# First projections of a hybrid backbone step: two blocks of 1024 channels and three column chunks, or four blocks of 512 and four chunks

## The chip, the cores and the metric

One NeuronCore of one Trainium2 chip runs the whole step in one launch. The metric is the device time of that launch in microseconds. TensorE (PE) multiplies into eight PSUM banks of 128 x 512 fp32, ScalarE (ACT) and VectorE (DVE) work between PSUM and the on-chip memory, GpSimd (POOL) and SyncE (SP) mainly issue DMAs; 16 DMA engines serve all queues.

## What is computed

Two sequences of 128 tokens (context and latent, `NS = 2`) go through one layer at D = 2048, in float32. Cut to what matters here:

```python
mod = silu(cvec) @ w_ada + b_ada            # 2048 x 12288, split in six: shift1, scale1, gate1, shift2, scale2, gate2
h = rmsnorm(x, g1) * (1 + scale1) + shift1
p = h @ w_in + b_in                          # 2048 x 8192: u (1024) | q | k | v (3 x 1024) | gate_A | gate_B (2 x 2048)
A = fourier(u) @ w_fourier;  B = attention(q, k, v, cached keys) @ w_na_o
x = x + gate1 * ((sigmoid(gate_A) * A + sigmoid(gate_B) * B) @ w_out)
x = x + gate2 * hierarchical_moe(modulate(x))    # 16 experts, 2048 -> 512 -> 2048
```

## The kernel before

**The weights' ring.** All of w_ada, w_in, w_na_o, w_fourier and w_out come in loads of 1 MB into `raw`, a ring of `RAW = 4` slots, in one fixed order (`ring_order`), issued by SP. A load waits until the slot four loads earlier is released (`slot_released`, on `raw_done`). There are two kinds. An ada load is consumed by PE directly: four fp32 products of the conditioning vectors with 512 columns each (`ada_block`, L685, for shift1 and scale1; `ada_super`, L701, for the four later sixths), 8 records in the trace. A dense load `l` is four rows-of-128 of a projection weight by 512 columns; ACT rounds it to fp32r (`high(u)`, L1257: `w_hi`), DVE takes the rest (`low(u)`, L1599: `w_lo = raw - w_hi`, which releases the slot after the second half), and PE multiplies in two units, `unit(l, 0)` and `unit(l, 1)`, of 12 matmuls each (three products L719 to L721 for two k and two sequences). `w_hi` and `w_lo` have four places (`AHEAD = 4`): high(u) waits for unit u - 4. A product adds up in a pair of PSUM banks over all loads of a chunk of 512 columns; then `read_chunk` on DVE (L1677) adds the bias row and writes it to `uqkv`.

**The first projections.** h needs shift1 and scale1, and these need every row of w_ada for their columns. The kernel before makes them in two blocks of 1024 channels: 16 ada loads, the evacuation of the rows (`modrow`, ACT, L1310), `mod_block` (PE turns the rows into columns, L734; DVE adds and scales), `modulate` (ACT, L1296, four instructions for four k of a sequence) and `split_h` (DVE, L1633 and L1634: h_hi and h_lo). While block 1's ada loads run, three to each dense load, the products of block 0 run: loads 0 to 5 are the two quads of k that are ready, for three column chunks (`P0_CHUNKS = 3`). The three sums stay open in six banks until loads 6 to 11 add the other half; each of these comes with one load of the later sixths (`ada_super`). From `L_MAIN = 12` on every chunk runs through its four quads, with one ada_super load to each dense load as long as there are any, and the rest hangs on `l`: attention heads at `HEAD_AT` (15, 17, 19, 21, 25, 27, 29, 31), the Fourier mixing at `DFT_AT` = 33, the columns of shift2 at DFT_AT + 6, the gates and merges from `L_MERGE` = 32, w_out from `L_OUT` = 80 to `L_ALL` = 96.

**After the ring** come the router and the 16 experts in eight pairs, whose loads (mraw) can begin when the ring's last dense loads are used up (SP waits on `unit_used`).

**POOL's queue** is a fixed list too: two bias rows of w_in (`load_bin`) once half of h is there (`h_ready` 4), then after `h_ready` 8 the relative-offset bias (eight small loads, `bias_rows` out to memory, four `bias` blocks back), two heads' cached keys and values (`cst`), and the further bias rows, each when the row before it in its place has been added.

## Time and profile before

| | us |
|---|---|
| Median of three runs | 1265.59 (1264.56 to 1265.74) |
| The profiled execution | 1263.68 |
| Its span, first to last instruction | 1261.9 |
| PE busy, DVE busy, ACT busy | 1156.0, 511.2, 373.8 |
| Moved by DMA | 423.27 MB |

Durations are of the profiled execution. A fp32 matmul has two records, and matmuls overlap, so that 24 matmuls of a dense load take less than 24 times the mean of one; times from start to start are the ones to add up.

### The profile page before, as it was taken

The numbers are of one execution on the slowest core, as the hardware profiler recorded it, in microseconds if no ns is written. First come the engines' busy times: TensorE is split into PE (matmuls) and PEld (weight loads), VectorE is DVE, ScalarE is ACT, GpSimd is POOL, SyncE is SP. The second block draws the span as 40 slices with busy tenths as digits, with TensorE's granted clock in tenths as the row PEclk, the third lists the DMA queues.
The fourth block names the chain that finished last, engine by engine and source line by source line (L and its number), as shares of the span: only waits on it lengthen the run. The fifth ranks groups of instructions, "written<-read, shape, count | busy, mean of one in ns | idle before, by whom it ended". The sixth has DMA issues, their size and how long they took to land.

```text
span 1261.9 us, 14226 instructions
## 1 busy us (share of the span) xinstructions
PE 1156.0 (92%) x5577; PEld 685.2 (54%) x5577; DVE 511.2 (41%) x722; ACT 373.8 (30%) x530; POOL 44.3 (4%) x81
## 2 busy tenths in 40 slices
PE   5779899999999999999999999999798889888785
PEld 2236567766766676778887784444233324333232
DVE  0022445545533445546456646125133323323046
ACT  3222424433332333334445534221021111201013
POOL 0000210010000300000000000000000000000000
PEclk9689899999999999999999999999999999999998
DMA  9999999888774998886565558999999999999998
GB/s 379 407 376 354 323 327 360 289 315 286 280 268 161 327 320 310 319 281 206 179 249 185 174 193 345 421 422 419 422 421 421 421 421 421 421 421 420 421 408 322
DMA packets 105955, 423.27 MB, mean 335 GB/s; under 512 B 8865, under 2 KB 9041, under 8 KB 73121
## 3 DMA queue, kind: packets, MB, share of 16 engines
q1 hardware_dynamic: 101264, 410.55, 84.8%
q0 software_dynamic: 4032, 11.22, 2.9%
q8 instruction: 45, 0.74, 0.2%
q10 hardware_dynamic: 592, 0.59, 0.1%
q14 instruction: 22, 0.17, 0.0%
HBM read 418.37 MB, written 3.95 MB: 335 GB/s over the span
## 4 chain that ended last, share of the span: by engine, by line
PE 69%; DMA 27%; DVE 1%; ACT 1%; issue 1%; SPq 0%; DVEq 0%; POOL 0%; ACTq 0%
PE bank L719 14%; PE bank L721 13%; PE bank L720 13%; PE bank L1086 11%; DMA raw<-in_w_ada 8%; DMA mraw<-in_w_exp_up 6%; DMA mraw<-in_w_exp_gate 5%; PE bank L701 4%; DMA mraw<-in_w_exp_down 4%; PE bank L1116 3%; DMA mraw_g<-in_w_exp_up 2%; PE bank L1027 2%; PE bank L685 2%; DMA mraw_g<-in_w_exp_down 1%; PE bank L1157 1%; PE bank L865 1%
## 5 line engine op out<-in xcount | busy, mean ns | idle before, releaser
L1599 DVE TENSOR_TENSOR w_lo<-raw,w_hi 128x1024 fp32r<-128x1024 f32 x192 | 233.6, 1224 | 273.7 <-ACT w_hi L1257 273.2
L1257 ACT ACTIVATE w_hi<-raw 128x1024 fp32r<-128x1024 f32 x192 | 201.9, 1058 | 312.8 <-PE bank L721 221.4
L1086 PE MATMUL bank<-mraw,xg 128*64 128x512 f32 x904 | 233.5, 601 | 18.2 <-DMA mraw<-in_w_exp_gate 8.0
L719 PE MATMUL bank<-w_hi,h_hi 128*128 128x512 f32 x512 | 210.7, 411 | 3.9 <-DVE w_lo L1599 3.9
L721 PE MATMUL bank<-w_hi,h_lo 128*128 128x512 f32 x512 | 201.4, 393 | 0.0
L720 PE MATMUL bank<-w_lo,h_hi 128*128 128x512 f32 x512 | 201.4, 393 | 0.0
L1086 PEld LDWEIGHTS bank<-mraw,xg 128*64 128x64 f32 x904 | 73.5, 137 | 137.3 <-issue 133.4
L1116 PE MATMUL bank<-mraw,hidT 128*64 128x512 f32 x408 | 101.1, 596 | 24.2 <-DMA mraw<-in_w_exp_down 22.0
L719 PEld LDWEIGHTS bank<-w_hi,h_hi 128*128 128x128 f32 x512 | 97.3, 190 | 47.5 <-issue 29.2
L721 PEld LDWEIGHTS bank<-w_hi,h_lo 128*128 128x128 f32 x512 | 97.2, 190 | 21.5
L720 PEld LDWEIGHTS bank<-w_lo,h_hi 128*128 128x128 f32 x512 | 97.5, 190 | 19.5 <-issue 1.0
L1545 ACT ACTIVATE d_hi<-bank,slot_w 128x512 fp32r<-128x512 f32 x32 | 22.0, 687 | 237.4 <-PE bank L1116 149.4
L2007 DVE SCALAR_TENSOR_TENSOR d_lo<-bank,slot_w,d_hi 128x512 fp32r<-128x512 f32 x32 | 23.9, 747 | 167.7 <-ACT d_hi L1545 167.0
L1116 PEld LDWEIGHTS bank<-mraw,hidT 128*64 128x64 f32 x408 | 32.5, 136 | 82.6 <-issue 75.9
L685 PE MATMUL bank<-raw,cpad 128*32 128x512 f32 x256 | 44.9, 789 | 32.9 <-DMA raw<-in_w_ada 32.9
L2019 DVE TENSOR_TENSOR bank<-bank,ga2b 128x512 f32<-128x512 f32 x64 | 41.5, 694 | 80.3 <-PE bank L1157 80.2
L701 PE MATMUL bank<-raw,cpad 128*32 128x512 f32 x512 | 67.4, 604 | 2.9 <-DMA raw<-in_w_ada 2.9
L1086 PE MATMUL bank<-mraw_g,xg 128*64 128x512 f32 x120 | 54.7, 598 | 3.2 <-DMA mraw<-in_w_exp_gate 3.1
L719 PE MATMUL bank<-w_hi,m_hi 128*128 128x512 f32 x128 | 51.5, 402 | 0.0
L721 PE MATMUL bank<-w_hi,m_lo 128*128 128x512 f32 x128 | 50.0, 391 | 0.0
L720 PE MATMUL bank<-w_lo,m_hi 128*128 128x512 f32 x128 | 49.9, 390 | 0.0
L1954 DVE TENSOR_TENSOR xg<-bank,rbi 128x512 f32<-128x512 f32 x32 | 21.9, 685 | 52.9 <-PE bank L1027 52.5
(260 smaller groups left out, 1140.7 us busy)
## 6 DMA issues: line engine op xcount, KB each, us to landing
raw<-in_w_in SPq DMA_DIRECT2D x64, 1024.0 KB, 5.8
raw<-in_w_ada SPq DMA_DIRECT2D x64, 1024.0 KB, 7.4
mraw<-in_w_exp_up SPq DMA_DIRECT2D x59, 1024.0 KB, 16.0
mraw<-in_w_exp_gate SPq DMA_DIRECT2D x58, 1024.0 KB, 16.0
mraw<-in_w_exp_down SPq DMA_DIRECT2D x51, 1024.0 KB, 16.0
raw<-in_w_ada SPq DMA_DIRECT2D x64, 512.0 KB, 7.9
raw<-in_w_out SPq DMA_DIRECT2D x16, 1024.0 KB, 5.0
raw<-in_w_na_o SPq DMA_DIRECT2D x8, 1024.0 KB, 5.4
```

Of the source, the lines that this page charges most:

```text
L685: last = nc.tensor.matmul(bank[7 - b % 2][32 * g:32 * g + 32], cpad[:, j], raw[:, n % RAW, g], start=j == 0, stop=j == KD - 1)
L701: last = nc.tensor.matmul(bank[7][32 * g:32 * g + 32], cpad[:, k], raw[:, n % RAW, g], start=k == 0, stop=k == KD - 1)
L719: nc.tensor.matmul(o, hi[:, k, s], wh, start=k == 0, stop=False)
L720: nc.tensor.matmul(o, hi[:, k, s], wl, start=False, stop=False)
L721: last = nc.tensor.matmul(o, lo[:, k, s], wh, start=False, stop=k == LOAD_K * quads - 1)
L1027: last = nc.tensor.matmul(out[:, kk * EPG * CAP:(kk + 1) * EPG * CAP], (t_hi, t_lo)[part][:, s, k * P:(k + 1) * P], pick[:, s, g * EPG:(g ...
L1086: last = nc.tensor.matmul(out[x * CAP:(x + 1) * CAP], xg[:, q * LOAD_K + kk, e * CAP:(e + 1) * CAP], slab(slot)[:, kk * COL:(kk + 1) * COL ...
L1116: last = nc.tensor.matmul(bank[first_bank + n][x * CAP:(x + 1) * CAP], hidT[:, i % 2, k, x * CAP:(x + 1) * CAP], slab(slot)[:, n * COL:(n ...
L1257: nc.scalar.activation(w_hi[:, u % AHEAD], r, ACT.Copy).then_inc(hi_ready, 1)
L1599: v.tensor_tensor(w_lo[:, u % AHEAD], r, w_hi[:, u % AHEAD].bitcast(F32), ALU.subtract).then_inc(raw_done[n % RAW], 4)
L2007: v.scalar_tensor_tensor(out=d_lo[:, c % 2], in0=bank[first_bank + n][:], scalar=slot_w[:, i:i + 1], in1=d_hi[:, c % 2].bitcast(F32), op0= ...
L2019: v.tensor_tensor(bank[out + s][:], bank[out + s][:], ga2b[:, s, cols], ALU.mult).then_inc(y_scaled, 1)
```

## The change

The first projections run in four blocks (`BLOCKS = 4`) of 512 channels, one quad of k each, for four column chunks (`P0_CHUNKS = 4`). A block takes 8 ada loads, each of two rows of k by 512 columns of shift1 and scale1 (the same 1 MB, in pieces of 2 KB where they were 4 KB). Between the blocks' dense loads (four to a block) stand the ada loads of the next block. Each dense load is now a sum of its own, opened and closed in a pair of banks; two pairs take turns, and `add_partial` on DVE adds it to `uqkv` in memory (the first with the bias row), 16 of these for the 16 dense loads. PE waits for the add of load l - 2 before load l. h of sequence 0 is modulated on ACT, that of sequence 1 on DVE. `L_MAIN` is 16; the number of loads in all stays the same, 96 ada and 96 dense. The heads follow one another without a break (17, 19, ... 31), the columns of shift2 come at 44, the evacuations of the later sixths 8 loads later, the mask is added at L_MAIN + 1 instead of L_MAIN + 3, and GpSimd loads four bias rows early (`xT_ready` 6). Counts of reads become `reads(chunk) = chunk + 1 + 12`.

```diff
-        P0_CHUNKS = 3
+        P0_CHUNKS, BLOCKS = 4, 4
         L_MAIN = 4 * P0_CHUNKS
-        L_MERGE = L_MAIN + 4 * 5
+        L_MERGE = L_MAIN + 4 * (8 - P0_CHUNKS)
         L_OUT = L_MERGE + 4 * 12
         L_ALL = L_OUT + 4 * 4
         A_SUPER = 32
-        A_MAIN = A_SUPER + 7
+        A_MAIN = A_SUPER + 3
...
-        ring_order = ["ada"] * 16 + ["ada", "ada", "ada", "dense"] * 5 + ["ada", "dense"]
-        ring_order += ["ada"] + ["ada", "dense"] * 6
+        ring_order = ["ada"] * 8 + ["dense"]
+        for b in range(BLOCKS - 1):
+            ring_order += ["ada", "ada", "ada", "dense"] * 2 + ["ada", "ada", "dense", "dense"]
+        ring_order += ["ada", "dense"] * 3
...
-            pair = chunk if chunk < P0_CHUNKS else (chunk - P0_CHUNKS) % 2
+            pair = (chunk + 1) % 2
             return 2 * pair, 2 * pair + 1
 
+        def reads(chunk):
+            return chunk + 1 + 3 * P0_CHUNKS
         def x1T_bank(n, s):
 
             return 1 if n == 3 and s else 6
 
-        HEAD_AT = [L_MAIN + 3 + 2 * h for h in range(4)] + [L_MAIN + 13 + 2 * h for h in range(4)]
+        HEAD_AT = [L_MAIN + 1 + 2 * h for h in range(8)]
         DFT_AT = HEAD_AT[7] + 2
+        SHIFT_AT = max(DFT_AT + 6, super_end(SHIFT2) + 2)
...
-                n = ADA_AT[16 * b + j]
+                n = ADA_AT[8 * b + j]
                 slot_released(n)
                 for m in (SHIFT1, SCALE1):
-                    sp.dma_start(raw[:, n % RAW, 2 * m:2 * m + 2].rearrange("p (a k) n -> p a (k n)", a=1),
-                                 ada_v[:, j:j + 1, m * D + b * 2 * COL:m * D + (b + 1) * 2 * COL]).then_inc(raw_landed[n % RAW], 16)
+                    sp.dma_start(raw[:, n % RAW, 2 * m:2 * m + 2],
+                                 ada_v[:, 2 * j:2 * j + 2, m * D + b * COL:m * D + (b + 1) * COL]).then_inc(raw_landed[n % RAW], 16)
...
-            for j in range(16):
+            for j in range(8):
                 ada_block_load(0, j)
-            for i in range(6):
-                for j in range(3 * i, min(3 * i + 3, 16)):
-                    ada_block_load(1, j)
-                dense_load(i)
-            ada_super_load(A_SUPER)
-            for i in range(6):
-                ada_super_load(A_SUPER + 1 + i)
-                dense_load(6 + i)
+            dense_load(0)
+            for b in range(1, BLOCKS):
+                for ch, js in ((1, (0, 1, 2)), (2, (3, 4, 5)), (3, (6, 7))):
+                    for j in js:
+                        ada_block_load(b, j)
+                    dense_load(P0_CHUNKS * (b - 1) + ch)
+                dense_load(P0_CHUNKS * b)
+            for i in range(3):
+                ada_super_load(A_SUPER + i)
+                dense_load(L_MAIN - 3 + i)
...
-            pool.wait_ge(h_ready, 4)
+            pool.wait_ge(xT_ready, 6)
             load_bin(0)
             load_bin(1)
+            load_bin(2)
+            load_bin(3)
             pool.wait_ge(h_ready, 8)
             load_bias_rows()
             load_cached_head(0)
             load_cached_head(1)
             skew_bias_rows()
-            load_bin(2)
-            load_bin(3)
...
-                n = ADA_AT[16 * b + j]
+                n = ADA_AT[8 * b + j]
                 if j == 0 and b == 1:
                     pe.wait_ge(vecT_ready, 1)
+                if j == 0 and b >= 2:
+                    pe.wait_ge(mod_ready, b - 1)
                 pe.wait_ge(raw_landed[n % RAW], landed_count(n))
                 for g in range(4):
-                    last = nc.tensor.matmul(bank[7 - b % 2][32 * g:32 * g + 32], cpad[:, j], raw[:, n % RAW, g],
-                                            start=j == 0, stop=j == KD - 1)
+                    last = nc.tensor.matmul(bank[7 - b % 2][32 * g:32 * g + 32], cpad[:, 2 * j + g % 2], raw[:, n % RAW, g],
+                                            start=j == 0, stop=j == 7)
...
-            def unit(l, half):
+            def unit(l, half, within=None):
 
                 chunk, quad, quads = chunk_of(l)
+                first, final = (LOAD_K * quad, LOAD_K * quad + 3) if l < L_MAIN else (0, LOAD_K * quads - 1)
...
+                    if t and within is not None:
+                        mod_block(within)
...
-                if quad == 0 and chunk >= P0_CHUNKS:
-                    pe.wait_ge(chunk_read, chunk - 2 if chunk < P0_CHUNKS + 2 else chunk - 1)
+                if l < L_MAIN:
+                    if l >= 2:
+                        pe.wait_ge(chunk_read, l - 1)
+                elif quad == 0:
+                    pe.wait_ge(chunk_read, reads(chunk - 2))
...
-            for j in range(1, 16):
+            for j in range(1, 8):
                 ada_block(0, j)
                 if j == 2:
                     pe.wait_ge(diag_ready, 1)
-                if 2 <= j < 10:
-                    if j >= 8:
-                        pe.wait_ge(xT_ready, j - 7)
-                    norm_transpose(x0, j - 2, bank[(j - 2) % 6])
+                if j >= 2:
+                    norm_transpose(x0, j - 2, bank[j - 2])
             mod_block(0)
-            for j in range(3):
-                ada_block(1, j)
-            for i in range(6):
-                for j in range(3 * i + 3, min(3 * i + 6, 16)):
-                    ada_block(1, j)
-                if i == 0:
-                    pe.wait_ge(xT_ready, 8)
-                    pe.wait_ge(h_ready, 2)
-                if i == 3:
-                    pe.wait_ge(h_ready, 4)
-                unit(i, 0)
-                if i == 5:
-                    mod_block(1)
-                unit(i, 1)
-            ada_super(A_SUPER)
-            ada_super(A_SUPER + 1)
-            for i in range(6):
-                ada_super(A_SUPER + 2 + i)
-                if i == 5:
-                    ada_super(A_SUPER + 8)
-                if i == 0:
-                    pe.wait_ge(h_ready, 6)
-                if i == 3:
-                    pe.wait_ge(h_ready, 8)
-                unit(6 + i, 0)
-                unit(6 + i, 1)
+            for b in (6, 7):
+                pe.wait_ge(xT_ready, b - 5)
+                norm_transpose(x0, b, bank[b - 6])
+            pe.wait_ge(xT_ready, 8)
+            def next_ada(b, js):
+                for j in js:
+                    if b < BLOCKS:
+                        ada_block(b, j)
+                    else:
+                        ada_super(A_SUPER + j)
+            for b in range(BLOCKS):
+                l = P0_CHUNKS * b
+                last_block = b == BLOCKS - 1
+                pe.wait_ge(h_ready, 2 * b + 2)
+                banks_free(l)
+                unit(l, 0)
+                next_ada(b + 1, (0,))
+                unit(l, 1)
+                next_ada(b + 1, (1,) if last_block else (1, 2))
+                banks_free(l + 1)
+                unit(l + 1, 0)
+                next_ada(b + 1, (2,) if last_block else (3,))
+                unit(l + 1, 1)
+                next_ada(b + 1, () if last_block else (4, 5))
+                banks_free(l + 2)
+                unit(l + 2, 0)
+                next_ada(b + 1, (3,) if last_block else (6,))
+                unit(l + 2, 1)
+                next_ada(b + 1, () if last_block else (7,))
+                banks_free(l + 3)
+                unit(l + 3, 0, None if last_block else b + 1)
+                next_ada(b + 1, (4,) if last_block else ())
+                unit(l + 3, 1)
...
+            def modulate(b):
                 for j in range(4):
-                    k = 4 * kg + j
-                    ins = nc.scalar.activation(htmp[:, buf, j], source(k, s, j), ACT.Identity,
-                                               bias=mod[:, sh, k, s:s + 1], scale=mod[:, g, k, s:s + 1])
+                    k = 4 * b + j
+                    ins = nc.scalar.activation(htmp[:, 0, j], xT[:, k, 0], ACT.Identity,
+                                               bias=mod[:, 0, k, 0:1], scale=mod[:, 1, k, 0:1])
                 ins.then_inc(htmp_ready, 1)
...
+            for n in range(6):
+                transposed(n)
+            for b in range(BLOCKS):
+                u = 2 * P0_CHUNKS * b
+                if b:
+                    high(u)
+                evac_block_rows(b)
+                if b:
+                    high(u + 1)
+                    act.wait_ge(h_ready, 2 * b)
                 act.wait_ge(mod_ready, b + 1)
-                act.wait_ge(xT_ready, 8)
-                for n in range(4 * b, 4 * b + 4):
-                    if n >= 2:
-                        act.wait_ge(h_ready, n - 1)
-                    modulate(n, lambda k, s, j: xT[:, k, s], 1, 0, 1, n % 2)
-                for u in range(12):
-                    high(12 * b + u)
+                modulate(b)
+                if b == 0:
+                    transposed(6)
+                    transposed(7)
+                    high(0)
+                    high(1)
+                for n in range(2, 2 * P0_CHUNKS):
+                    high(u + n)
...
+            def modulate(b):
+                dve.wait_ge(xT_ready, 2 * b + 2)
+                dve.wait_ge(mod_ready, b + 1)
+                for j in range(4):
+                    k = 4 * b + j
+                    ins = v.tensor_scalar(htmp[:, 1, j], xT[:, k, 1], mod[:, 1, k, 1:2], mod[:, 0, k, 1:2],
+                                          ALU.mult, ALU.add)
+                chained(ins)
...
+            def add_partial(l):
+                chunk, quad, _ = chunk_of(l)
+                col = PROJ_COLS[chunk]
+                dve.wait_ge(unit_used, 2 * l + 2)
+                if quad == 0:
+                    dve.wait_ge(bin_landed[chunk % 2], 16 * (chunk // 2) + 16)
+                else:
+                    dve.wait_ge(chunk_read, l - P0_CHUNKS + 1)
+                for s, b in enumerate(banks_of(chunk)):
+                    total = uqkv[:, s, col:col + COL]
+                    ins = v.tensor_tensor(total, bank[b][:], total if quad else bin_[:, chunk % 2], ALU.add)
+                ins.then_inc(chunk_read, 1)
...
-            for b in range(2):
+            for b in range(BLOCKS):
+                l = P0_CHUNKS * b
+                if b:
+                    low(2 * l)
+                    add_partial(l - 2)
                 mod_block(b)
-                for n in range(4 * b, 4 * b + 4):
-                    split_h(n, n)
-                for u in range(12):
-                    low(12 * b + u)
-            for n in range(AHEAD):
-                low(2 * L_MAIN + n)
-                if n < P0_CHUNKS - 1:
-                    read_chunk(n)
+                modulate(b)
+                split_h(b, 1)
+                dve.wait_ge(htmp_ready, b + 1)
+                split_h(b, 0)
+                if b:
+                    low(2 * l + 1)
+                    add_partial(l - 1)
+                else:
+                    low(0)
+                    low(1)
+                for ch in range(1, P0_CHUNKS):
+                    low(2 * (l + ch))
+                    low(2 * (l + ch) + 1)
+                    if ch >= 2:
+                        add_partial(l + ch - 2)
+            low(2 * L_MAIN)
+            low(2 * L_MAIN + 1)
+            add_partial(L_MAIN - 2)
+            low(2 * L_MAIN + 2)
+            low(2 * L_MAIN + 3)
...
-                if l == L_MAIN + 3:
+                if l == L_MAIN + 1:
                     add_mask()
                 if l == L_MAIN:
-                    read_chunk(P0_CHUNKS - 1)
+                    add_partial(L_MAIN - 1)
```

## Rows read from the trace of the kernel before

**Rows 1.** The page, part 1: busy us, share of the span, instructions.

```profile
PE 1156.0 (92%) x5577; PEld 685.2 (54%) x5577; DVE 511.2 (41%) x722; ACT 373.8 (30%) x530; POOL 44.3 (4%) x81
```

**Rows 2.** Stretches: busy us per engine (instructions), then PEclk, DMA share, GB/s.

```profile
13.00:35.00 22.00, 18.77 (x113) 8.26 (x113) 1.64 (x8) 7.18 (x12) 0.00 (x0) 1.00 1.03 409
...
43.00:74.00 31.00, 21.87 (x97) 4.54 (x98) 7.30 (x15) 8.75 (x19) 1.09 (x2) 0.56 1.02 391
74.00:133.00 59.00, 49.53 (x257) 30.95 (x257) 18.32 (x25) 18.86 (x30) 1.19 (x3) 0.96 0.92 350
...
200.00:757.00 557.00, 555.61 (x2679) 411.26 (x2682) 284.45 (x351) 223.10 (x280) 28.99 (x50) 1.00 0.74 258
757.00:1262.00 505.00, 439.65 (x2098) 182.31 (x2090) 170.79 (x297) 90.81 (x166) 0.00 (x0) 0.99 0.99 409
```

**Rows 3.** Timeline of PE: start, us, line, operation, idle before it and releaser.

```profile
13.59 1.93 PE L685 MATMUL bank<-raw,cpad 128*32 128x512 f32 x8 [13.59 <-DMA raw<-in_w_ada]
...
66.10 1.06 PE L685 MATMUL bank<-raw,cpad 128*32 128x512 f32 x8 [3.04 <-DMA raw<-in_w_ada]
...
73.70 0.80 PE L719 MATMUL bank<-w_hi,h_hi 128*128 128x512 f32 x1
...
132.80 0.77 PE L719 MATMUL bank<-w_hi,h_hi 128*128 128x512 f32 x1 [3.87 <-DVE w_lo L1599]
...
186.75 1.07 PE L701 MATMUL bank<-raw,cpad 128*32 128x512 f32 x8 [1.84 <-DMA raw<-in_w_ada]
```

**Rows 4.** Timeline of PE, two successive products with w_ada between dense units.

```profile
141.24 1.06 PE L701 MATMUL bank<-raw,cpad 128*32 128x512 f32 x8
...
147.90 1.07 PE L701 MATMUL bank<-raw,cpad 128*32 128x512 f32 x8
```

**Rows 5.** Stretches after the hole before 132.80; the clock is the third from last.

```profile
132.00:136.00 4.00, 3.20 (x8) 2.56 (x9) 3.79 (x4) 2.23 (x3) 4.00 (x9) 0.50 0.84 289
136.00:138.00 2.00, 2.00 (x6) 1.57 (x5) 0.36 (x1) 0.00 (x0) 2.00 (x5) 0.50 0.95 319
138.00:140.00 2.00, 2.00 (x8) 1.60 (x7) 0.00 (x0) 0.61 (x1) 1.01 (x2) 0.81 1.08 427
```

**Rows 6.** DMA: packets of the stretch 59:62, and the main queue in 560:600.

```profile
DMA packets 524, 1.17 MB, mean 390 GB/s; under 512 B 18, under 2 KB 18, under 8 KB 523
...
q1 hardware_dynamic: 3934, 7.80, 60.0%
```

**Rows 7.** Timeline of ACT: evacuation of 128x512, modulation, w_hi of a dense load.

```profile
40.09 0.60 ACT L1303 ACTIVATE xT<-bank 128x512 f32<-128x512 f32 x1 [1.97 <-PE bank L755]
...
58.52 1.65 ACT L1296 ACTIVATE htmp<-xT,mod 128x128 f32<-128x128 f32 x4 [2.67 <-DVE mod L1648]
...
132.84 2.00 ACT L1257 ACTIVATE w_hi<-raw 128x1024 fp32r<-128x1024 f32 x2 [0.61 <-DMA raw<-in_w_in]
```

**Rows 8.** Timeline of DVE: scaling, one split of h, w_lo of a load, a chunk's two adds.

```profile
17.48 0.61 DVE L1622 TENSOR_SCALAR diag<-cst_all,rms 128x128 f32<-128x128 f32 x2
...
78.40 2.36 DVE L1599 TENSOR_TENSOR w_lo<-raw,w_hi 128x1024 fp32r<-128x1024 f32 x2 [10.16 <-ACT w_hi L1257]
...
130.36 0.43 DVE L1633 CAST h_hi<-htmp 128x512 fp32r<-128x512 f32 x1 [0.39 <-ACT htmp L1296]
130.82 0.69 DVE L1634 TENSOR_TENSOR h_lo<-htmp,h_hi 128x512 fp32r<-128x512 f32 x1
...
170.35 1.28 DVE L1677 TENSOR_TENSOR uqkv<-bank,bin 128x512 f32<-128x512 f32 x2
```

**Rows 9.** SP's queue: the issue of the dense load that the w_hi at 132.84 reads.

```profile
127.28 0.38 SPq L462 DMA_DIRECT2D raw<-in_w_in  x1
```

**Rows 10.** Waits for the heads' cached keys (us, times), POOL's timeline, landing (the page, last column).

```profile
  DMA cst<-in_cache_v_ctx: 6.2, 5
...
141.88 1.14 POOL L575 DMA_DIRECT2D bias_rows<-rpbpad  x1 [2.87 <-DMA rpbpad<-in_rpb]
...
bias_rows<-rpbpad POOLq DMA_DIRECT2D x1, 768.0 KB, 11.6
```

76 lines of the change are left out of this document (34 added, 42 removed).

## The prediction

> **What bounds the kernel now.** I read the page first: TensorE (PE) is busy 92% of 1261.9 us and VectorE 41% [rows 1]. A share over the whole span decides nothing here, so the table by stages comes next [rows 2]. From 757 us to the end the 16 DMA engines are full at 409 GB/s: the experts' weights arrive as fast as they can, and this stage starts when the one before it ends. From 200 to 757 us PE is busy 555.6 of 557 us at full clock, with DMA at 74%. So whatever the first stages win or lose reaches the end undiminished. Up to 133 us it is the other way round: DMA at 92 to 103%, PE idle for a part and granted 0.56 of its clock from 43 to 74 us. PE's own rows show why [rows 3]: the first product of the projections starts at 73.70 us, when 22 of the 32 block loads of w_ada have been multiplied; the second half of h then costs another hole of 3.87 us before 132.80. From 132.80 on PE runs back to back, apart from 1.84 us at 186.75.
>
> **The yardstick.** From 133 us on a pair of one w_ada product and one dense load takes 6.66 us (141.24 to 147.90), of which the w_ada load is 1.0 and the dense load's 24 matmuls are 5.65 [rows 4]. At 132.80 us the kernel before has 6 dense loads, 32 block loads and 3 of the later w_ada loads behind it. In the changed kernel the comparable point is the first unit of the last channel block, unit(12, 0): 12 dense loads and 32 block loads are behind it, and PE should be full from there. It is six dense loads further and three w_ada loads less far: 33.9 - 3.0 = 30.9 us. Before also runs at half clock from 132.80 to 138.8 (the stretches 132:136 and 136:138 show 0.50 and 138:140 shows 0.81), which costs 3.0 us more [rows 5]. So the change breaks even if unit(12, 0) starts at 132.8 + 3.0 + 30.9 = 166.7 us. Everything below is about that one time.
>
> **Part by part.** (1) Half the w_ada loads before the first h: 8 instead of 16. Each is now 2 KB pieces where it was 4 KB. With 4 KB pieces and full queues DMA moves 409 GB/s (13:35), 2.56 us for a load of 1.05 MB [rows 2]. For 2 KB pieces there are two bounds. With a full queue, the stretch 59:62, which holds the first w_in load, moves 390 GB/s, so 1.05 MB takes 2.7 us; loads of w_in issued one at a time (560:600) use 60.0% of the engines for 7.80 MB in 40 us, 325 GB/s or 3.2 us a load [rows 6]. I take 2.8, nearest to the full queue in which most of these loads stand, and keep 2.7 and 3.3.
> The first product at 13.59 us moves by 0.3, seven more loads take 19.6, and the two bias rows of 0.26 MB that GpSimd now loads this early are 1.3 us of DMA, of which I count half, 0.7: the eighth lands at 34.2 and is multiplied by 35.3. The chain behind it is priced by its rows: evacuation 0.65, mod_block 1.0 (as many passes as a w_ada product), mod 0.4 (two instructions on 8 and 16 numbers, bounded by 0.61 for two on 128), four ScalarE modulations 1.6 [rows 4, 7, 8]; the two late transposes are evacuated (1.2) and the first w_hi made (1.05), while VectorE modulates the other sequence (1.25), splits both (1.15 each) and makes the first w_lo (1.2). First unit at 42.6 instead of 73.70 us.
> (2) The start of the first block. PE has had a hole of over 3 us there, and both holes of 3.0 and 3.87 us in the old kernel were followed by half clock [rows 3, 5]; so 6 us of half clock, 3.0 lost.
> (3) The ring of four slots. Every load waits for the slot four loads back. After unit(4b, 1) the first freed slots are those of w_ada products 1 and 2, and loads 4 and 5 and then the dense load of chunk 2 come through them. A load issued into an empty queue landed 5.56 us after its issue (127.28 to 132.84) [rows 7, 9]; I take 5.4. From the block's start: product 1 is done at 7.75 (two units 5.65, two products 2.1), load 4 lands at 13.15, load 5 at 15.95, the dense load at 18.75.
> (4) Closed sums. 12 more pairs of adds, 1.28 us a pair [rows 8], 15.4 us of VectorE in all, beside PE's work. What is on the path is their place: add_partial(l-2) stands behind both low() of load l, and unit(l, 0) waits for it because of the banks. From landing to that unit it is w_hi 1.06, 0.95 and w_lo 1.2, add 1.3 and the waits: 4.8 us, against 2.3 with w_hi and w_lo alone. Where PE is the limit this is hidden: two units and two or three products (7.7 us or more) run meanwhile. Where the load is late, it is paid. Queued behind the adds on VectorE are only w_lo of later loads and, at a block's start, mod and h.
> So unit(4b+2, 0) starts 18.75 + 4.8 = 23.55 us after the block, while PE, with two units and three products more, is ready at 17.6: a hole of 6 us. After it half clock again; I charge 2.5 us. Then two units and two products (7.75), and unit(4b+3) with mod_block in it (3.75 + 2.8 = 6.6). The block takes 23.55 + 7.75 + 2.5 + 6.6 = 40.4 us. DMA needs 12 x 2.8 = 33.6 of these, PE 32.1: neither is the bound, the handing on between them is.
> (5) At the boundary the new h is ready 4.05 us after mod_block (0.4 + 1.25 + 2 x 1.15 and waits), and PE has 4.2 us of work left: nothing, or up to 1 us a block.
> (6) First block: a dense load that is there already, 3.0 us lost at the start; the same working gives unit(2, 0) at 69.3 and unit(4, 0) at 86.15. With two more blocks unit(12, 0) comes at 86.15 + 80.8 = 166.95: +0.25 against break-even.
> (7) Two more mod_blocks are in these times. Later moves: the heads stand two loads apart without the break after four, so one more head meets its cached keys late (6.2 us over 5 such waits, +1.2 [rows 10]); the loads of bias rows 2 and 3 leave the crowded stretch in which the 1.84 us hole lay: -0.9, bounds 0 and -1.8. add_mask comes two loads sooner while the bias is ordered later: GpSimd's chain from the last h (131.5) to the issue of bias_rows at 141.88 is 10.4 us, its landing 11.6, and as much again with its issue for the four bias blocks, 34 to 38 us in all; VectorE gets there after about 37 (five dense loads and six w_ada products, 34.3, and w_hi and w_lo), and PE needs it 6 us later; nothing, at most 3 [rows 8, 10]. The later shifts of mod_super, gate rows and router weights have 8 loads or more of room.
> Sum: 0.25 + 1.2 - 0.9 = +0.6 us on the profiled execution's 1263.7, so 1264.3; the median is 1.9 above that execution: **1266**.
>
> **A rule of the notes.** Holes of 3.0 and 3.87 us here were followed by half clock, those of 1.8 us or less weren't [rows 3, 5]. The Trainium skill (TensorE: Matmul & The Clock Gate, "HAM oscillation — how this bites in real kernels") tells of a kernel that waits for its next slice at every step and restarts slow each time; by that, three blocks with a 6 us hole each pay each time, which is what the forecast has, and without it there would be 161.4 instead of 166.95. The same skill (DMA: Bandwidth & Descriptors, "Anatomy of one DMA") puts some 2 us of a DMA's time in the confirmation that its last byte is written, whatever its size, for GpSimd's path; by that a load into an empty queue would take about 2 + 2.7 = 4.7 us (an estimate from that page), and the blocks 0.7 us less each; the trace's 5.56 decides.
>
> **Rivals.** A, the clock stays full through the holes: the block takes 38.55 (then the dense load of chunk 3 sets it), unit(12, 0) at 161.4, -5.0 in all: 1260.6. For it: the holes of 1.8 us cost no clock; against: 3.87 did. B, the queue is better fed than my hand-on says, because loads land in less than 5.4 behind one another: DMA-bound blocks of 33.6 to 35, unit(12, 0) at 146 to 151, -15 to -20: 1246 to 1251. For it: DMA stands at 1.02 from 43 to 74 us in spite of the same four slots [rows 2]; against: there at most one dense load in four had to be waited for. C, slower: 2 KB loads run at 3.3 us because the queue is shallow; then the first h comes 3.5 later, the first block 1.0 and each of the next two 1.0 more: +6.5, 1272.7. It decides from about 3.0 us a load on; the 325 GB/s row speaks for it, the 390 GB/s row against. With up to 1 us a boundary from (5) on top, 1275. D, the adds aren't late and nothing moves, because the first blocks aren't on the path: excluded by PE's full 557 us.
>
> **How the numbers follow.** Forecast with its own range of 1263 to 1269: 0.33. A: 0.22. B or half of it: 0.15. C: 0.30. D: 0. What a measurement can tell from no change is about 0.2%, 2.5 us. The forecast's case gives same 0.26, slower 0.04, faster 0.03; A faster 0.19, same 0.03; B faster 0.15; C slower 0.27, same 0.03. So faster 0.37, same 0.32, slower 0.31. The range leaves out a full B and what may lie beyond C: 1252, just above B's 1251, to C's 1275 with the boundary waits.
>
> **What would show it.** First unit at 42.6 (+-1.5); in each of three blocks a hole of 6 us ahead of unit(4b+2, 0) that ends with w_lo and adds, and half clock after it; blocks of 40 us; unit(12, 0) at 167; 2 KB loads 2.8 us apart in the first 34 us; no hole over 2 us from there to 757; the adds after 133 us never ahead of a PE wait. Wrong would be: holes under 3 us (B), blocks of 38.5 with full clock (A), loads 3.3 us apart (C).

## The result and the profile after

The changed kernel takes 1271.61 us (median of 5 runs, 1270.25 to 1272.31) against 1265.74 for the kernel before beside it: ratio 1.0042, interval 1.0027 to 1.0056. On another chip, 12 runs gave 1270.59 against 1264.38, again 1.0042 (1.0027 to 1.0058). So it is slower by some 6 us. The forecast was 1266, in a range of 1252 to 1275; slower had a chance of 0.31, less than faster's 0.37. The profiled execution took 1271.73 us with a span of 1269.9, which is 8.0 longer than before's.

The page, part 1 (columns as in [rows 1]): PE has 2.5 us more to do, VectorE 18. The shares hardly move and tell nothing.

```profile
PE 1158.5 (91%) x5593; PEld 689.6 (54%) x5593; DVE 529.5 (42%) x760; ACT 368.4 (29%) x516; POOL 44.4 (3%) x81
```

PE's timeline of the changed kernel (columns as in [rows 3]). The three products at the end are single dense loads far behind the changed part, with nothing between them.

```profile
43.69 0.77 PE L734 MATMUL bank<-w_hi,h_hi 128*128 128x512 f32 x1 [3.05 <-DVE w_lo L1637]
...
69.80 0.79 PE L734 MATMUL bank<-w_hi,h_hi 128*128 128x512 f32 x1 [6.36 <-DVE uqkv L1719]
...
110.55 0.80 PE L734 MATMUL bank<-w_hi,h_hi 128*128 128x512 f32 x1 [6.51 <-DVE uqkv L1719]
...
150.79 0.79 PE L734 MATMUL bank<-w_hi,h_hi 128*128 128x512 f32 x1 [6.08 <-DVE uqkv L1719]
...
186.72 1.06 PE L713 MATMUL bank<-raw,cpad 128*32 128x512 f32 x8 [1.49 <-DMA raw<-in_w_ada]
...
202.47 1.06 PE L713 MATMUL bank<-raw,cpad 128*32 128x512 f32 x8 [2.36 <-DMA raw<-in_w_ada]
...
617.14 0.39 PE L734 MATMUL bank<-w_hi,h_hi 128*128 128x512 f32 x1
...
622.59 0.39 PE L734 MATMUL bank<-w_hi,h_hi 128*128 128x512 f32 x1
...
628.02 0.39 PE L734 MATMUL bank<-w_hi,h_hi 128*128 128x512 f32 x1
```

The first unit starts at 43.69 where before had 73.70 [rows 3]. Then each of the three blocks has one hole of over 6 us, always before unit(4b+2, 0), and always ended by the add of L1719. How one of them comes about stands in the timelines of SP's queue, ACT and DVE.

```profile
90.22 5.85 SPq L445 DMA_DIRECT2D raw<-in_w_ada  x6
96.26 0.37 SPq L469 DMA_DIRECT2D raw<-in_w_in  x1
...
105.78 2.00 ACT L1283 ACTIVATE w_hi<-raw 128x1024 fp32r<-128x1024 f32 x2 [11.07 <-DMA raw<-in_w_in]
...
106.94 2.36 DVE L1637 TENSOR_TENSOR w_lo<-raw,w_hi 128x1024 fp32r<-128x1024 f32 x2 [10.71 <-ACT w_hi L1283]
109.22 1.28 DVE L1719 TENSOR_TENSOR uqkv<-bank,uqkv 128x512 f32<-128x512 f32 x2
```

SP issues the dense load at 96.26, when its slot is free. It has landed when w_hi begins at 105.78, behind the w_ada pieces. Two w_hi, two w_lo and only then the add follow, and PE goes on at 110.55: 4.8 us from landing to unit. The add's operands had been ready for long; it stands behind the w_lo that wait for the load.

Stretches of the changed kernel (columns as in [rows 2]): a hole, what follows it, the crowded stretch after the blocks and what follows that, then the rest of the ring.

```profile
104.00:111.00 7.00, 0.49 (x5) 0.45 (x2) 3.56 (x4) 2.00 (x2) 0.00 (x0) 0.82 1.05 387
111.00:116.00 5.00, 5.00 (x16) 3.55 (x19) 0.91 (x1) 2.01 (x2) 0.00 (x0) 0.57 0.80 294
...
186.00:204.00 18.00, 14.93 (x74) 9.82 (x75) 7.87 (x11) 4.01 (x4) 3.84 (x6) 1.00 1.04 355
204.00:208.00 4.00, 4.00 (x12) 3.10 (x11) 2.14 (x3) 1.06 (x1) 0.00 (x0) 0.57 0.97 377
208.00:757.00 549.00, 547.11 (x2647) 398.72 (x2646) 277.60 (x342) 219.18 (x274) 28.54 (x49) 1.00 0.76 267
```

From 208 us on PE is full at full clock, as before [rows 2]. So what is lost before 208 us reaches the end. The second hole after the blocks has GpSimd's DMAs beside it. POOL's timeline and SP's queue, and in a fence of its own the table of DMA issues of 175:205 (its last column is us from issue to landing):

```profile
175.45 1.14 POOL L584 DMA_DIRECT2D bias_rows<-rpbpad  x1 [0.43 <-DMA rpbpad<-in_rpb]
187.75 2.73 POOL L593 DMA_DIRECT2D bias<-bias_rows  x4 [11.16 <-DMA bias_rows<-rpbpad]
190.48 1.12 POOL L606 DMA_DIRECT2D bin<-in_b_in  x2
...
194.50 0.34 SPq L453 DMA_DIRECT2D raw<-in_w_ada  x1
```

```profile
raw<-in_w_ada SPq DMA_DIRECT2D x5, 1024.0 KB, 12.8
```

The w_ada load issued at 194.50 meets the bias blocks and the two bias rows, which GpSimd had issued by 191.6, and lands at 202.4. The five w_ada loads of this stretch take 12.8 us from issue to landing; from 208 to 300 us, beside smaller DMAs of GpSimd, they take 7.4.

The starts of loads 15, 16 and 17 of the changed kernel, in PE's timeline:

```profile
190.56 0.39 PE L734 MATMUL bank<-w_hi,h_hi 128*128 128x512 f32 x1
...
197.23 0.39 PE L734 MATMUL bank<-w_hi,h_hi 128*128 128x512 f32 x1
...
207.91 0.40 PE L734 MATMUL bank<-w_hi,h_hi 128*128 128x512 f32 x1
```

**The ledger**, at the last dense matmul of the ring: 754.32 before, 761.95 after, +7.6. The blocks give +2.9 (below). Before lost a little less behind 132.80 than the 3.0 that this +2.9 charges it: its load 6 took 9.43 us (132.80 to 142.23) where a pair takes 6.67, and two w_ada products next to each other saved it 0.2: +0.45. Load 16 of the changed kernel takes 10.68 us where load 15, with the same work in it, takes 6.67: the hole and the half clock behind it, +4.0. The one old hole is 1.49 instead of 1.84, and 0.15 comes back beside it: -0.2. At the heads PE waits 0.88 and 1.01 us for cached keys where it waited 1.39: +0.5. That is +7.65, the whole. The span's +8.0 is at the high end: the medians differ by 5.9 and 6.2, and executions of one kernel spread over 2 to 10.5 us.

### The profile page after: what moved, and what is told of

The parts are those of the page before. It is cut to its first block, busy times and chain, and to the rows that moved or that the text cites. A ratio compares the mean times of both kernels' runs of the same rounds, so it can differ in the third digit from the quotient of the medians.

```text
span 1269.9 us, 14313 instructions
## 1 busy us (share of the span) xinstructions
PE 1158.5 (91%) x5593; PEld 689.6 (54%) x5593; DVE 529.5 (42%) x760; ACT 368.4 (29%) x516; POOL 44.4 (3%) x81
## 4 chain that ended last, share of the span: by engine, by line
PE 67%; DMA 28%; DVE 2%; issue 1%; ACT 1%; SPq 1%; POOL 0%; DVEq 0%
PE bank L734 14%; PE bank L736 13%; PE bank L735 13%; PE bank L1112 10%; DMA mraw<-in_w_exp_gate 6%; DMA mraw<-in_w_exp_up 6%; PE bank L713 4%; DMA raw<-in_w_ada 4%; DMA mraw<-in_w_exp_down 4%; PE bank L1142 3%; DMA raw<-in_w_in 3%; DMA mraw_g<-in_w_exp_up 2%; PE bank L1053 2%; DMA mraw_g<-in_w_exp_down 1%; DMA cst<-in_cache_v_ctx 1%; PE bank L891 1%
## 5 line engine op out<-in xcount | busy, mean ns | idle before, releaser
L1637 DVE TENSOR_TENSOR w_lo<-raw,w_hi 128x1024 fp32r<-128x1024 f32 x192 | 233.5, 1224 | 286.1 <-ACT w_hi L1283 285.7
L734 PE MATMUL bank<-w_hi,h_hi 128*128 128x512 f32 x512 | 214.8, 420 | 22.4 <-DVE uqkv L1719 19.0
L1142 PEld LDWEIGHTS bank<-mraw,hidT 128*64 128x64 f32 x408 | 32.5, 136 | 81.1 <-issue 74.4
L713 PE MATMUL bank<-raw,cpad 128*32 128x512 f32 x512 | 68.0, 604 | 4.9 <-DMA raw<-in_w_ada 4.9
L697 PE MATMUL bank<-raw,cpad 128*32 128x512 f32 x256 | 35.7, 646 | 16.5 <-DMA raw<-in_w_ada 16.5
```

Of the source, the lines that this page charges most:

```text
L697: last = nc.tensor.matmul(bank[7 - b % 2][32 * g:32 * g + 32], cpad[:, 2 * j + g % 2], raw[:, n % RAW, g], start=j == 0, stop=j == 7)
L713: last = nc.tensor.matmul(bank[7][32 * g:32 * g + 32], cpad[:, k], raw[:, n % RAW, g], start=k == 0, stop=k == KD - 1)
L734: nc.tensor.matmul(o, hi[:, k, s], wh, start=k == first, stop=False)
L1142: last = nc.tensor.matmul(bank[first_bank + n][x * CAP:(x + 1) * CAP], hidT[:, i % 2, k, x * CAP:(x + 1) * CAP], slab(slot)[:, n * COL:(n ...
L1637: v.tensor_tensor(w_lo[:, u % AHEAD], r, w_hi[:, u % AHEAD].bitcast(F32), ALU.subtract).then_inc(raw_done[n % RAW], 4)
```

## The experiments

Line numbers in the diffs are left out; L1719 and L1637 shift by a few where lines are added. "Unit(12, 0)" and "last matmul" (the last dense matmul of the ring) are starts in the profiled execution: 167.6 and 761.95 in the changed kernel, 754.32 for the latter before. Ratios are to the kernel before on the same chip.

**1 and 2, the adds and the order of PE's work.** First theory: a block's hole is the late load plus an add in the wrong place. Rival: the load alone sets it, and the adds are hidden behind it. The first kernel moves the add ahead of the split that waits for the load; the second lets PE multiply the w_ada loads that have landed before it starts the dense unit, so that slots come free sooner.

```diff
-                    low(2 * (l + ch))
-                    low(2 * (l + ch) + 1)
                     if ch >= 2:
                         add_partial(l + ch - 2)
+                    low(2 * (l + ch))
+                    low(2 * (l + ch) + 1)
```

> The changed kernel with one thing moved: on VectorE each closed sum's add stands ahead of the two w_lo of the load that waits for its banks, instead of behind them. Theory H (handing on): the hole of 6.1 to 6.5 us ahead of unit(4b+2, 0) is made of late landing plus w_hi, w_hi, w_lo, add; with the add made while the load is still under way, only landing, w_hi and one w_lo are left, so each of the three holes shrinks by about 2.5 us to 3.9, first h unchanged, unit(12, 0) at about 160 instead of 167.6, and 7.5 us less in all (about 1264). The half clock behind each hole stays, since a hole of 3.87 us had it too. Rival D (it is the transfer, DMA being the bound of the blocks): holes and time stay within 1 us. Rival V (VectorE has too many adds to do): the same work in another order, so nothing moves either.

```diff
+                next_ada(b + 1, () if last_block else (0, 1) if b == 0 else (0, 1, 2))
                 pe.wait_ge(h_ready, 2 * b + 2)
                 banks_free(l)
                 unit(l, 0)
-                next_ada(b + 1, (0,))
+                next_ada(b + 1, (0,) if last_block else (2,) if b == 0 else ())
                 unit(l, 1)
-                next_ada(b + 1, (1,) if last_block else (1, 2))
+                next_ada(b + 1, (1,) if last_block else ())
```

> The changed kernel with the first three products of the next block's w_ada loads made ahead of a block's first unit instead of between its units (in block 0 two ahead; last block as it was). Theory H: slots of the ring come free some 7 us sooner, so loads 4, 5 and the dense load of chunk 2 land 3 us or more sooner (the second of them then waits for its own slot, that of chunk 1's load); each hole shrinks by about 3 us, and unit(12, 0) comes 8 to 9 us sooner: about 1263. It also fills the hole ahead of the very first unit with products. Rival D (2 KB loads are simply slow, 3.2 us each): DMA was busy anyway, the loads land when they did, within 1 us of the changed kernel.

The first: 1266.69 us (10 runs), 1.0016 (1.0001 to 1.0032), unit(12, 0) at 161.8, last matmul at 756.73. The second: 1267.26 (10 runs), 1.0013 (1.0001 to 1.0025), 161.9 and 756.49. PE's timeline of the first and, below the dots, of the second:

```profile
69.17 0.76 PE L734 MATMUL bank<-w_hi,h_hi 128*128 128x512 f32 x1 [4.10 <-DVE w_lo L1637]
106.35 0.64 PE L734 MATMUL bank<-w_hi,h_hi 128*128 128x512 f32 x1 [2.96 <-DVE w_lo L1637]
```

```profile
66.74 0.80 PE L734 MATMUL bank<-w_hi,h_hi 128*128 128x512 f32 x1 [5.86 <-DVE uqkv L1720]
106.49 0.80 PE L734 MATMUL bank<-w_hi,h_hi 128*128 128x512 f32 x1 [5.27 <-DVE uqkv L1720]
```

With the add first, the releaser becomes w_lo. From the landing (the start of w_hi, 66.65, 103.82 and 142.16) to the unit it is 2.5 us in each block instead of 4.8: the unit now waits for one w_lo only, where it stood behind the second w_lo (1.1) and the add (1.3). The holes shrink by 2.3, 3.5 and 1.5 us; what differs from 2.3 comes from when the load lands and when PE runs out of work. With the products first the add still ends the hole, 4.8 us behind the landing, but the load lands 17.4, 14.8 and 13.9 us after the block's first unit instead of 21.3, 19.5 and 18.9, and the holes are 5.86, 5.27 and 4.29. Both causes are real: by the ratios, taking either away brings the time 3 to 4 us nearer to before's.

**3, GpSimd's loads out of the crowded stretch.** Theory: the second hole after the blocks is a collision of GpSimd's bias DMAs with the ring. Rival: the ring alone makes it. The bias loads are issued before the wait for the last h.

```diff
             load_bin(3)
-            pool.wait_ge(h_ready, 8)
             load_bias_rows()
-            load_cached_head(0)
-            load_cached_head(1)
             skew_bias_rows()
             load_bias_blocks()
+            pool.wait_ge(h_ready, 8)
+            load_cached_head(0)
+            load_cached_head(1)
```

> The changed kernel with GpSimd's relative-offset bias (eight small loads, bias_rows out, four bias blocks back) issued behind the bias rows of the first block instead of behind the last h. Theory C (collision): the holes of 1.49 us at 185 and 2.36 us at 200, and the 3.4 us of half clock behind the second, come from these DMAs and two bias rows beside the ring; without them the stretch from unit(12, 0) to unit(17, 0) is 4 to 5 us shorter; the first blocks, where DMA has room, get at most 1 us longer: about 1267.5. Rival: the ring falls short there by itself after the last block, because its slots come free late: then both holes stay and nothing moves.

1272.61 us (4 runs), 1.0061 (1.004 to 1.0083). The collision is confirmed and the place was wrong. Load 16 takes 6.7 us instead of 10.68 and the clock stays full there; from unit(12, 0) to unit(17, 0) it is 36.4 us, where the eight profiled executions of four-block kernels that leave GpSimd's queue alone take 38.6 to 41.0. Only a hole of 1.66 is left there, but block 1 takes 47.7 us (85.3 to 133.0) and unit(12, 0) is at 173.7: now PE waits twice more for w_ada inside the block. PE's timeline, and the stretch after load 16:

```profile
100.31 1.42 PE L697 MATMUL bank<-raw,cpad 128*32 128x512 f32 x8 [2.78 <-DMA raw<-in_w_ada]
108.93 1.06 PE L697 MATMUL bank<-raw,cpad 128*32 128x512 f32 x8 [2.03 <-DMA raw<-in_w_ada]
...
203.00:208.00 5.00, 5.00 (x27) 3.21 (x25) 3.16 (x5) 2.12 (x2) 0.00 (x0) 1.00 0.86 323
```

**4, the size of the pieces.** Each block load of w_ada takes one row of 4 KB per partition instead of two of 2 KB, the same bytes; the modulation so uses other numbers than the reference's.

```diff
-                    sp.dma_start(raw[:, n % RAW, 2 * m:2 * m + 2],
-                                 ada_v[:, 2 * j:2 * j + 2, m * D + b * COL:m * D + (b + 1) * COL]).then_inc(...)
+                    sp.dma_start(raw[:, n % RAW, 2 * m:2 * m + 2].rearrange("p (a k) n -> p a (k n)", a=1),
+                                 ada_v[:, j:j + 1, m * D + b * COL:m * D + (b + 2) * COL]).then_inc(...)
```

> The changed kernel with the block loads of w_ada read as one row of 1024 columns (4 KB pieces) instead of two rows of 512; the same 1 MB a load and the same instructions elsewhere, but the numbers are not the ones needed, so the modulation is wrong. It asks what the 2 KB pieces cost alone. Theory H: products with full queues 2.56 us apart instead of 2.70, first unit 1.0 to 1.3 us sooner, each block 0.3 to 0.8 us shorter, 2 to 3.5 us in all (about 1269). Rival C of the forecast (2 KB pieces in a shallow queue are the loss): blocks shorter by 3 us each, about 1261.

1270.92 us (10 runs, 1266.25 to 1274.14), 1.0047 (1.0029 to 1.0065): no gain. Its profiled execution is the fastest of the ten; there the first w_ada products come 2.56 us apart instead of 2.71, unit(12, 0) comes at 162.9 and the first unit at 41.3, 1.1 to 2.4 earlier than in the five profiled executions with 2 KB and the same order of work up to there (42.4 to 43.7). So the trace shows a small effect, about 1.2 us over eight loads with a full queue, that the medians don't show: inconclusive for the whole, and no evidence that the pieces cause the loss.

**5, both orders together.** The diffs of 1 and 2 in one kernel.

> The changed kernel with both: adds ahead of the two w_lo, and the next block's first products ahead of a block's first unit. Theory H: the two act on different parts of one chain (the slots' release at its beginning, the add at its end), so they add up. With the products first alone the holes were 5.86, 5.27 and 4.29 us; with the add off the path each loses 2.5 us more, to 3.4, 2.8 and 1.8; the shorter ones keep the clock. unit(12, 0) at 152 to 155, about 1257 to 1260, faster than the kernel before by 0.4 to 0.6%. Rival D (the transfer becomes the bound as soon as the hand-on is shorter; the 12 loads of a block need 33.6 us): the blocks stay at 36 us or more, the second measure brings 2 us at most: 1264 or more.

1260.67 us (10 runs), 0.997 (0.9956 to 0.9984), faster than before. Unit(12, 0) is at 157.7, the last matmul at 749.86. The largest holes left in the blocks, in PE's timeline:

```profile
77.18 1.05 PE L752 MATMUL bank<-cst_all,modrow 128*128 128x4 f32 x8 [2.69 <-ACT modrow L1337]
...
103.70 0.77 PE L734 MATMUL bank<-w_hi,h_hi 128*128 128x512 f32 x1 [2.83 <-DVE w_lo L1638]
```

Both are under 3 us, and in the blocks half clock is left only at 42.1 to 48.9 and 103.5 to 107.0. Behind the blocks a hole of 2.07 us before 177.37 is followed by 3.5 us of half clock; the one in load 16 is 0.70 here, with GpSimd's queue unchanged.

**6, GpSimd's loads in the kernel before.** What the same move does where there are no closed sums: all bias DMAs are issued ahead of the wait for h_ready 8.

```diff
-            pool.wait_ge(h_ready, 8)
             load_bias_rows()
-            load_cached_head(0)
-            load_cached_head(1)
             skew_bias_rows()
-            load_bin(2)
-            load_bin(3)
             load_bias_blocks()
+            pool.wait_ge(h_ready, 8)
+            load_cached_head(0)
+            load_cached_head(1)
+            load_bin(2)
+            load_bin(3)
```

> The kernel before with GpSimd's relative-offset bias issued at once instead of behind the last h, as a control. Theory C (collision): its hole of 1.84 us at 186.75 is due to these DMAs too and goes. But in the first 50 us DMA is full and the first h waits for 16 loads, so 1.3 MB more there cost 3 us: about +1 in all, 1266.5. Rival: the hole is the ring's own and stays; then +3.

1266.59 us (10 runs), 1.0018 (1.0006 to 1.0029). The hole of 1.84 us of [rows 3] is gone, the pairs there are 6.67 us apart:

```profile
181.49 1.07 PE L701 MATMUL bank<-raw,cpad 128*32 128x512 f32 x8
188.16 1.07 PE L701 MATMUL bank<-raw,cpad 128*32 128x512 f32 x8
```

But the first unit starts at 74.8 instead of 73.70, unit(6, 0) at 136.7 instead of 132.80 and the last matmul at 756.06 instead of 754.32: in that kernel's first 133 us GpSimd's bytes are in the way of the ring.

**7, the clock apart from the holes.** Five products of constants into a bank that isn't read, after products 4 and 5 of each of the first three blocks, keep PE at work in the hole.

```diff
                 next_ada(b + 1, () if last_block else (4, 5))
+                if not last_block:
+                    spare_products(5)
```

> The changed kernel with five further fp32 products of 128 x 512 into an unused bank behind the products 4 and 5 of the first three blocks, that is at the start of the hole of 6 us; they compute nothing that is used and take 5.6 us. It asks what the half clock behind the holes costs. Theory K (the hole's length decides on the clock): the holes shrink to under 1 us, the clock stays full in the blocks, the 4.5 to 5.4 us at half clock behind each hole lose no more 2.3 to 2.7 us; some of it comes back as a wait for the dense load of chunk 3: 1.5 to 2 us a block, 5 in all, about 1266.5. Rival: the clock falls as before, by another cause than the hole; then nothing is won and up to 1 us a block is lost.

1268.48 us (10 runs, 1262.67 to 1272.4), 1.0033 (1.0012 to 1.0053). Stretch 43:168 of the kernel before, the changed one and this one (the clock is third from last), each with its own row:

```profile
43.00:168.00 125.00, 106.41 (x508) 60.17 (x512) 39.43 (x51) 38.66 (x59) 9.44 (x17) 0.85 0.97 362
```

```profile
43.00:168.00 125.00, 104.56 (x506) 65.80 (x507) 53.25 (x78) 31.89 (x41) 1.29 (x3) 0.90 0.87 309
```

```profile
43.00:168.00 125.00, 118.48 (x574) 70.62 (x573) 56.33 (x81) 33.70 (x43) 8.27 (x16) 0.99 0.92 325
```

The clock stays full from 47.0 to 801 us: the half clock after each hole comes from the hole, not from the kind of work that follows. What it is worth can't be told. The profiled execution, the fastest of ten, has unit(12, 0) at 160.3, but the interval of the medians overlaps the changed kernel's.

**8, the bias loads spread out.** The kernel of 5, with bias_rows issued early, its skew after h_ready 6 and the blocks after h_ready 8.

```diff
             load_bin(3)
-            pool.wait_ge(h_ready, 8)
             load_bias_rows()
-            load_cached_head(0)
-            load_cached_head(1)
+            pool.wait_ge(h_ready, 6)
             skew_bias_rows()
+            pool.wait_ge(h_ready, 8)
             load_bias_blocks()
+            load_cached_head(0)
+            load_cached_head(1)
```

> As e5, and GpSimd's bias spread out: its eight small loads behind the bias rows, bias_rows out when the third block's h is there (the ring's DMAs rest for 3 to 5 us at a block's start), the four blocks and the cached keys behind the last h. Theory C: bias_rows in the fixed place of e3 struck while loads were being waited for and cost a block 6 us; here it meets the rest of the ring and costs under 1 us, and the stretch from unit(12, 0) to unit(17, 0) loses its holes and the half clock, 4 us: 3 us less than e5. Rival: the collision in l = 13 to 16 is with the bias blocks and bias rows 4 and 5, which stay there: same as e5 within 1 us.

1265.11 us (10 runs), 1.0015 (1.0001 to 1.0029): 4 us slower than the kernel of 5. POOL's timeline:

```profile
119.96 1.14 POOL L584 DMA_DIRECT2D bias_rows<-rpbpad  x1 [49.19 <-DVE h_lo L1672]
```

This one DMA of 768 KB is followed by a hole of 5.93 us before 133.96, and unit(12, 0) comes 6 us later than in 5. Behind the blocks load 16 takes 6.7 us at full clock, as hoped, but a hole of 2.02 is left at 176, and the gain there doesn't pay for the loss in the block.

**9, the changed kernel once more,** beside 10 and 11 on their chip, to see what repeats.

> The changed kernel once more, unaltered, on the chip of the two others of this call, since the runs of one kernel spread over 3 to 8 us and the comparisons with it went over chips so far. Every theory: 1.004 of the kernel before, within 0.15%; in its trace the three holes of about 6 us with half clock behind them, unit(12, 0) at 167 +- 1.5, and a hole with 3.4 us of half clock between unit(14, 0) and unit(17, 0). If the landings differ from execution to execution, that last hole is the first to come and go.

Its times stand at the top. Its profiled execution is the slowest of its twelve (1274.7): unit(12, 0) at 169.8, holes of 7.92, 7.19 and 6.45, each at the same place as in the first trace, and again a second hole after the blocks, of 2.06, with 3.4 us of half clock behind it. PE's timeline:

```profile
72.57 0.79 PE L734 MATMUL bank<-w_hi,h_hi 128*128 128x512 f32 x1 [7.92 <-DVE uqkv L1719]
```

**10 and 11, toward a better kernel.** The tenth is the kernel of 5 with ScalarE evacuating a block's rows for mod_block before it makes w_hi, and the add of a block's first load moved as well. The eleventh has bias rows 4 and 5 issued after h_ready 4 in addition.

```diff
                 if b:
-                    high(u)
                 evac_block_rows(b)
                 if b:
+                    high(u)
                     high(u + 1)
...
                 if b:
-                    low(2 * l)
                     add_partial(l - 2)
+                    low(2 * l)
```

> e5 with the block boundary freed of the next dense load: ScalarE evacuates the w_ada rows before the first w_hi of the new block, and VectorE adds l - 2 before its w_lo. In e5 PE waited 2.69 and 1.66 us for these rows in the middle of unit(4b+3), because ScalarE stood at a w_hi whose load had not landed. Theory H: both waits go and mod comes 1.3 us or more sooner at each of three boundaries; 2 to 4 us less than e5, 1257 to 1259. Rival D (the blocks are at DMA's bound now, 34 to 38 us each): what is won at the boundary is waited for at the next dense load, under 1 us.

```diff
             load_bin(3)
+            pool.wait_ge(h_ready, 4)
+            load_bin(4)
+            load_bin(5)
             pool.wait_ge(h_ready, 8)
...
             load_bias_blocks()
-            load_bin(4)
-            load_bin(5)
```

> e10 with bias rows 4 and 5 of w_in (0.5 MB) loaded when the second block's h is there, instead of behind the bias blocks. Theory C: the collision between unit(13, 0) and unit(17, 0) (2.07 us of hole and 3.4 us at half clock in e5) is one of the sum of GpSimd's DMAs in 25 us, so half a megabyte less shortens the hole by 1.3 us and lets the clock stay: 2 to 3.5 us less than e10. Rival: bias_rows alone with its 11 to 12 us makes it; then nothing moves there.

The tenth: 1259.7 us (11 runs), 0.9966 (0.9945 to 0.9988), unit(12, 0) at 154.4, last matmul at 746.80. The waits for modrow are gone; against the kernel of 5 the trace shows 3.1 us, the ratios 0.5, which is within their uncertainty. The eleventh: 1258.23 us (11 runs), 0.995 (0.9934 to 0.9967), last matmul at 746.89, and load 16 takes 7.6 us instead of 9.0. PE's timeline of the tenth, then of the eleventh:

```profile
189.65 1.06 PE L713 MATMUL bank<-raw,cpad 128*32 128x512 f32 x8 [2.25 <-DMA raw<-in_w_ada]
```

```profile
175.39 1.06 PE L714 MATMUL bank<-raw,cpad 128*32 128x512 f32 x8 [1.56 <-DMA raw<-in_w_ada]
...
189.68 1.06 PE L714 MATMUL bank<-raw,cpad 128*32 128x512 f32 x8 [0.85 <-DMA raw<-in_w_ada]
```

The 2.25 us hole is 0.85 when two rows of 0.26 MB each leave the stretch. That pair of numbers alone shows nothing, since 5 had 0.70 there with the rows in place; the whole stretch from unit(12, 0) to unit(17, 0) is 37.4 us, below all eight with the queue unchanged, 39.1 in the tenth. In the blocks the eleventh is 1.7 later (unit(12, 0) at 156.1), so the last matmuls stand level, and the 1.5 us between the medians are within their uncertainty. The eleventh has the lowest median here, 6.2 us faster than before and 12.4 faster than the changed one on the same chip.

## Why the prediction was right and where it was wrong

**The blocks: right.** First unit 43.69 (forecast 42.6), w_ada loads 2.71 apart (2.8), unit(2, 0) 69.80 (69.3), unit(4, 0) 86.3 (86.15), holes of 6.36, 6.51 and 6.08 (6), landing to unit 4.8 (4.8), blocks of 40.8 and 40.5 (40.4), unit(12, 0) 167.6 (166.95). In the first block two misses cancel: it began 1.1 late, and the half clock at its start, to 47.0, cost some 1.7 and not 3.0. Half clock follows each hole, 4.5 to 5.4 us of matmuls or 2.3 to 2.7 us lost (2.5). In step (4) the 17.6 us at which PE is ready hold four products, not the three that the text says; PE was ready after 17.8 and 17.6 in the second and third block. Experiments 1, 2 and 5 show that the hole has the two causes that the steps (3) and (4) name, and 7 that the clock follows the hole. By the rule of the Trainium skill (TensorE: Matmul & The Clock Gate, "HAM oscillation — how this bites in real kernels") each restart would be slow again; the stretch 111:116 at 0.57 agrees.

**The yardstick: the step that failed first.** It split a pair of 6.66 us into 1.0 for the w_ada product and 5.65 for the dense load, with the 1.0 read from a product's own row. A dense load alone takes 5.44 (617.14 to 622.59 to 628.02), so a w_ada product put between two costs 1.23. The comparison is six dense loads against three products, so the error doesn't cancel: break-even is 132.8 + 3.0 + 6 x 5.44 - 3 x 1.23 = 164.75, not 166.7. Unit(12, 0) at 167.6 is then +2.9 and not +0.25; 2.0 of the difference is the yardstick, 0.65 the time itself. The 3.0 for before's half clock was 0.45 too much as well (the ledger).

**After the blocks: the larger miss.** Step (7) took -0.9 because bias rows 2 and 3 leave the crowded stretch, and "no hole over 2 us from there to 757" was among the signs. What stays in it, the bias blocks and rows 4 and 5, I priced at nothing for the ring: I only asked when add_mask would need the bias, not which load its transfer would meet. There was a hole of 2.36 us with half clock behind it: +4.0, and -0.2 for the old hole. Experiments 3, 8 and 11 show that GpSimd's DMAs make most of what is lost there: with a part of them moved, unit(12, 0) to unit(17, 0) takes 36.4, 37.3 and 37.4 us instead of 38.6 to 41.0. Five dense loads and six w_ada products at 5.44 and 1.23 would take 34.6 (an estimate from these prices). No move of them brought a gain in the median that stands clear of the uncertainty. The ring's loads are late at one point of each block, and GpSimd's DMAs there cost more than they had behind the blocks (3 and 8).

**The heads:** +0.5 for +1.2, right in kind. add_mask, put at nothing, ran at 210.42 without a stall.

**The rivals.** A, full clock through the holes: the trace has 0.57. B, a better fed queue: the holes were as forecast, and even experiment 10 reaches only 154.4. C, 2 KB loads at 3.3 us: the result lies near its 1272.7, but not by its mechanism; the loads came every 2.71 us, and 4 KB pieces gave no gain in the medians. The time came 5.6 above the forecast: 2.65 from the blocks (+2.9 for +0.25), 0.45 from before's half clock, 4.7 from behind the blocks (+3.8 for -0.9), -0.7 from the heads and 0.35 after the ring that I can't place, some 7.4 in all. Against it stand 1.9 that I added to go from execution to median; the changed kernel's median is 0.1 below its execution. So the forecast's own range, 1263 to 1269 with a chance of 0.33, was missed; the wide range holds the result because it was stretched to 1275 for C, whose mechanism didn't occur. That part is luck.

**What stays open:** what the pieces of 2 KB cost in the blocks, for which trace and medians of 4 disagree; what the half clock alone is worth in the median; and why executions of one kernel reach unit(12, 0) up to 2.2 us apart (167.6 and 169.8).

## What to carry to other kernels

Where a ring of a few slots is fed by DMA and drained by work of several engines, neither the bytes nor the matmuls need be the bound: here a block needs about 32.5 us of DMA (12 loads at 2.71) and 32.6 of PE (four dense loads at 5.44, eight w_ada products at 1.23 and 1.0 for mod_block; both estimates from the measured prices) and takes 40, because each load waits for a slot and each unit for a chain of w_hi, w_lo and add behind its landing. So put an add that only needs finished products ahead of work that waits for a load, consume what has landed before work that frees no slot, and leave small transfers of other queues out of the stretches where the ring is late. When two schedules are compared by a yardstick, take the price of each item from a stretch where it stands alone.

## What the runs showed of the hardware that I had not expected

A w_ada product of 1.06 us costs 1.23 between dense units; the first dense matmul behind one takes 0.50 us and not 0.39.

Holes of 2.36 us here, 2.06 in the repeated run and 2.07 in experiment 5 were followed by 3.4 to 3.6 us of half clock; one of 2.25 in experiment 10, another of 2.11 in the repeated run and the 1.84 of [rows 3] were not. A hole's length alone so doesn't tell whether the clock falls. What does is open.

While one DMA of 768 KB for bias_rows was under way (175 to 187 us, 12.0 from issue to landing), the ring's w_ada and w_in loads took 12.0 and 12.8 us from issue to landing; from 208 to 300 us they took 7.4 and 5.5.
